# Differential attention on one Trainium2 core: all copies of turned weights on ScalarE, in the order in which TensorE makes them

## What is computed

```python
s = einsum('bqhcd,bkhcd->bchqk', q_blk, k) * scale     # c: two score maps per head
mask = cid[None, :] <= c_blk[:, None]
p = softmax(where(mask, s, NEG_INF), axis=-1)
w = p[:, 0] - lam * p[:, 1]
o = einsum('bhqk,bkhe->bqhe', w, v)                    # 4 heads, v is 128 wide
```

## Time and profile before

| | |
|---|---|
| median of 3 runs | 2430.82 us |
| the profiled execution | 2428.37 us |
| its span, first to last instruction | 2426.5 us |
| TensorE busy | 2216.3 us (91%) |
| VectorE busy | 783.8 us (32%) |
| ScalarE busy | 474.7 us (20%) |
| GpSimd busy | 308.9 us (13%) |
| mean granted clock of TensorE | 0.952 |

### The profile page before, as it was taken

The page is one execution under the profiler, slowest core; times in us unless marked ns, Lnnn a source line. Parts: engine busy times, 40 slices in busy tenths (PEclk is TensorE's granted clock), DMA queues, the critical chain, the costliest instruction groups (busy, mean ns, idle before and its releaser), DMA issues. The chain is left out here.

```text
span 2426.5 us, 33639 instructions
## 1 busy us (share of the span) xinstructions
PE 2216.3 (91%) x13491; PEld 1256.3 (52%) x13491; DVE 783.8 (32%) x1658; ACT 474.7 (20%) x885; POOL 308.9 (13%) x263
## 2 busy tenths in 40 slices
PE   8999997779949999999967999999976999999994
PEld 5778554555535545454434555555544554545541
DVE  7642245554361111111126344444243111111116
ACT  2222243331101000000003444441110000000001
POOL 7252000001101111111002000000101111101102
PEclk9999997889969999999988999999987999999998
DMA  4100001011259999989979111102119999999987
GB/s 154 37 36 1 20 1 70 1 33 43 69 202 399 420 419 420 416 337 409 411 300 309 51 39 39 32 11 53 56 53 392 416 417 420 420 376 372 417 367 297
DMA packets 148201, 529.82 MB, mean 218 GB/s; under 512 B 43875, under 2 KB 66947, under 8 KB 131665
## 3 DMA queue, kind: packets, MB, share of 16 engines
q1 hardware_dynamic: 127040, 493.66, 51.4%
q0 software_dynamic: 13312, 33.84, 3.7%
q10 hardware_dynamic: 7696, 0.19, 0.2%
HBM read 499.99 MB, written 39.98 MB: 223 GB/s over the span
## 5 line engine op out<-in xcount | busy, mean ns | idle before, releaser
L1864 PE MATMUL l_main_pgu<-l_w_ring,l_ex_xT 128*64 128x256 f32 (+1 forms) x4992 | 472.2, 384 | 11.3 <-DMA l_w_ring<-in_l_moe_w_gate 9.2
L1864 PEld LDWEIGHTS l_main_pgu<-l_w_ring,l_ex_xT 128*64 128x64 f32 (+1 forms) x4992 | 284.9, 128 | 187.9 <-issue 38.5
L1910 PE MATMUL l_main_py<-l_w_ring,l_ex_hT 128*64 128x512 f32 (+1 forms) x1248 | 231.9, 594 | 1.9 <-DVE l_ex_hT L1981 1.9
L1861 PE MATMUL l_main_pgu<-l_w_ring,l_ex_xT 128*128 128x512 f32 x384 | 170.1, 596 | 5.0 <-DMA l_w_ring<-in_l_moe_w_gate 5.0
L1977 DVE TENSOR_TENSOR l_ex_hid<-l_ex_sil,l_main_pgu 128x256 f32<-128x256 f32 (+1 forms) x76 | 35.2, 464 | 374.9 <-PE l_main_pgu L1864 277.7
L1981 DVE COPY l_ex_hT<-l_main_ph 128x256 f32<-128x256 f32 (+1 forms) x76 | 35.5, 467 | 366.4 <-PE l_main_ph L1885 366.4
L2322 PE MATMUL lru_pr<-h2T,lru_wz 128*128 128x352 f32 (+1 forms) x480 | 143.5, 459 | 10.8 <-ACTq L2377 10.8
L2340 PE MATMUL lru_pg<-h2T,lru_wz 128*128 128x512 f32 x320 | 148.7, 592 | 0.0
L1910 PEld LDWEIGHTS l_main_py<-l_w_ring,l_ex_hT 128*64 128x64 f32 (+1 forms) x1248 | 69.1, 127 | 132.1 <-issue 124.8
L2322 PEld LDWEIGHTS lru_pr<-h2T,lru_wz 128*128 128x128 f32 x480 | 92.1, 192 | 63.2 <-ACTq L2377 11.2
L1953 ACT ACTIVATE l_ex_sil<-l_main_pgu 128x256 f32<-128x256 f32 (+1 forms) x76 | 31.8, 418 | 468.2 <-PE l_main_pgu L1864 372.3
(11 more groups left out here) (459 smaller groups left out, 2810.6 us busy)
## 6 DMA issues: line engine op xcount, KB each, us to landing
l_w_ring<-in_l_moe_w_gate SPq DMA_DIRECT2D x64, 2048.0 KB, 24.8
l_w_ring<-in_l_moe_w_up SPq DMA_DIRECT2D x64, 2048.0 KB, 30.2
l_w_ring<-in_l_moe_w_down SPq DMA_DIRECT2D x64, 2048.0 KB, 31.7
l_y<-expert_rows SPq DMA_DIRECT2D x32, 512.0 KB, 8.1
h_rows<-H SPq DMA_DIRECT2D x24, 512.0 KB, 5.4
lru_wz<-in_l_w_in SPq DMA_DIRECT2D x20, 512.0 KB, 4.9
w_in<-in_l_w_in SPq DMA_DIRECT2D x4, 2048.0 KB, 9.5
H<-h_rows SPq DMA_DIRECT2D x16, 512.0 KB, 10.0
```

Of the source, the lines that this page charges most:

```text
L1861: last = pe.matmul(out[:], x[:, k, :], w[0][:, k, :], start=k == 0, stop=k == KD - 1)
L1864: last = pe.matmul(out[HALF * h + o:HALF * h + o + m, 0:256], x[:, k, it.at + o:it.at + o + m], w[n][:, k, 256 * h:256 * h + 256], start=k ...
L1910: last = pe.matmul(py[b][HALF * h + o:HALF * h + o + m, :], hT[:, c % 2, HALF * (c // 2) + o:HALF * (c // 2) + o + m], ws[n][:, c, 512 * h ...
```

## The change

The order of work changes in three places, all in `attention`:

- The copies leave VectorE. ScalarE makes every copy, group after group in the order in which TensorE turns them, with one semaphore (`w_copied`). Its round is now: copy of group 0 of unit u-1, first exponential of unit u+1, copy of group 1, second exponential, copy of group 2, `out(u-2)`.
- A copy is one instruction for the whole group. Where the group holds key tile 0, it copies 128 rows of that tile too, 112 of which were never written by a turn; so VectorE clears the first 128 columns of `turned_w` once at the start, and `meta_scores` waits for that (`tp_cleared`).
- v's products of a round stand all between the first `turn` and the first `weigh`; none stands before the `turn`.

```diff
             def meta_scores():
+                pe.wait_ge(tp_cleared, 1)
...
             def turn(u, j):
                 if n:
-                    pe.wait_ge((turned_a, turned_v)[(n - 1) % 2], (n - 1) // 2 + 1)
+                    pe.wait_ge(w_copied, n)
...
             def weigh(u, j):
-                pe.wait_ge((turned_a, turned_v)[n % 2], n // 2 + 1)
+                pe.wait_ge(w_copied, n + 1)
...
-                middle = (v_until[u + 1] + v_until[u + 2]) // 2
-                v_products(v_until[u + 1], middle)
                 for j in range(max(groups)):
                     if 0 <= u - LAG + 1 < U and j < groups[u - LAG + 1]:
                         turn(u - LAG + 1, j)
                     if j == 0:
-                        v_products(middle, v_until[u + 2])
+                        v_products(v_until[u + 1], v_until[u + 2])
...
+            def copy_turned(u, j):
+                if not (0 <= u < U and j < groups[u]):
+                    return
+                qi = units[u][1]
+                m, n = TILES[qi][1], first_group[u] + j
+                act.wait_ge(turned, n + 1)
+                if u >= 2:
+                    act.wait_ge(o_ready, u - 1)
+                k0, k1 = PER * j, min(PER * j + PER, qi + 1)
+                keys = P if k1 > 1 else N_META
+                act.copy(wT[u % 2][0:keys, k0:k1, 0:m], tp[0:keys, 0:k1 - k0, 0:m]).then_inc(w_copied, 1)
...
             for u in range(-1, U + LAG):            # ScalarE
-                if u + 1 < U:
-                    exps(u + 1, 0)
-                if 0 <= u - LAG + 1 < U:
-                    copies(act, act.copy, u - LAG + 1, 0, turned_a)
-                if u + 1 < U:
-                    exps(u + 1, 1)
+                for j in range(max(groups)):
+                    copy_turned(u - LAG + 1, j)
+                    if u + 1 < U and j < 2:
+                        exps(u + 1, j)
...
             do(dve.memset(ss[:], 0.0), wait=False)   # VectorE
+            dve.memset(tp[:, 0, :], 0.0).then_inc(tp_cleared, 1)
             do(dve.memset(o_sb[:, 0, :], 0.0))
...
                 if 0 <= u < U:
                     combine(u)
-                if 0 <= u - LAG + 1 < U:
-                    copies(dve, dve.tensor_copy, u - LAG + 1, 1, turned_v)
                 if 0 <= u - LAG - 1 < U:
                     square(u - LAG - 1)
```

More of the change, by code:

```diff
@@ L706, in attention @@
     sem = lambda n: K.sem("da_" + n)
-    (lexp_done, s_ready, mn_ready, exp_done, w_ready, turned, turned_a, turned_v, o_ready, o_copied,
+    (lexp_done, s_ready, mn_ready, exp_done, w_ready, turned, w_copied, tp_cleared, o_ready, o_copied,
      squared, dve_order, tail_done, tail_made, v_ready, v_copied) = map(sem, (
-        "lexp_done", "s_ready", "mn_ready", "exp_done", "w_ready", "turned", "turned_a",
-        "turned_v", "o_ready", "o_copied", "squared", "dve_order", "tail_done", "tail_made", "v_ready", "v_copied"))
+        "lexp_done", "s_ready", "mn_ready", "exp_done", "w_ready", "turned", "w_copied",
+        "tp_cleared", "o_ready", "o_copied", "squared", "dve_order", "tail_done", "tail_made", "v_ready", "v_copied"))
     ms_ready, sd_ready, on_ready, oT_ready, oT_copied = map(sem, ("ms_ready", "sd_ready", "on_ready", "oT_ready", "oT_copied"))
@@ L846, in _ @@
                 last.then_inc(oT_ready, 1)
[L848 to L865, removed]
         @block.scalar
```

## The result

The changed kernel takes 2368.61 us, the median of four runs (2363.71 to 2371.58), beside 2430.18 us before: ratio 0.9744, 95% interval 0.9722 to 0.9766. The profiled execution took 2371.58 us with a span of 2369.5, so it is 57.0 us shorter than the span before; the sum of the prediction said 51.7.

What follows compares the result with a forecast made beforehand. The order of work was taken as the bound, with TensorE waiting at `turn` in attention's long rounds. -33.4 + 2.2 - 21.0 + 0.2 + 0.3 = -51.7 us from 2428.4; 2379 us against the median, range 2371 to 2398.

Steps and rivals of the forecast that it cites:

- The waits at `turn`: Attention: with copies in TensorE's order, its waits for VectorE's and ScalarE's copies go, 28.8 + 4.6 = 33.4 us.
- ScalarE next: Rounds scoring 1040-key units: ScalarE is late next, TensorE waits for the exponential and `out`, 2.2 us added (0 to 3.6).
- VectorE: Attention: VectorE loses its copies, is not waited for afterwards, so this is worth nothing by itself.
- The low clock: Long rounds: low clock behind waits mostly goes, 22.7 us saved, 1.7 kept behind v's last copy, net 21.0 (0 to 24.2).
- The rival from the Trainium skill: Attention: short idle moments between matmul groups keep the clock falling, 21 us not gained; clock staying low: 2400 us, chance 0.12.
- The floor: Long rounds: TensorE's busy time at full clock, 109.4 - 22.7 = 86.7 us for 18 rounds, 4.8 us each.
- v's products: Short rounds: moving these products behind the turn is an exchange on TensorE's own list and costs nothing.
- The clearing: Start of attention: `meta_scores` waits for one more memset, clearing part of `turned_w`; 0.3 us added (0 to 0.6).
- What follows: After attention: w_out's load still has 90 us, so everything later moves up as a block.
- v's copy: End of the short rounds: the 1.9 us wait for the last copy of v stays, 0.2 us added as TensorE arrives sooner.

Runs made afterwards that it cites:

- copies alone moved: The changed kernel with v's products split again, half before the first turn and half behind it; 2373.41 us, ratio 0.9787 to the kernel before.
- v's copy moved up: The changed kernel with ScalarE's copy of a finished v tile behind the round's first exponential instead of behind `out`; 2365.45 us, again 2366.78 us.
- shared copies: The changed kernel with copies by turns on ScalarE and VectorE, each at its place in TensorE's order; 2385.45 us, ratio 0.9816 to the kernel before.
- exponential first: The changed kernel with unit u+1's exponential ahead of unit u-1's copy on ScalarE, all copies still there; 2391.75 us, ratio 0.985 to the kernel before.
- copies before the weights: The kernel before with VectorE's copies ahead of the next unit's weights, still behind both minima; 2395.01 us, ratio 0.9867.
- v's products moved: The kernel before with only v's products moved, all behind the first turn; 2426.03 us, ratio 0.9994.

## Why the prediction was right or wrong

**The waits at `turn`: right.** 33.4 us were to go and 33.35 went; no turn waits for a copy any more (one weighing of the last short units waits 0.4 us for one). The prediction put too much on the long waits, though: it had the low windows all "behind waits of 2 us and more", and four of the eleven, from 376.33, 383.15, 441.18 and 506.04 us, stood behind waits of 1.92, 1.45, 1.79 and 1.91 us. The two sides of the theory were tested apart: the order by turning ScalarE's list round, and the engine by sharing the copies again.

**ScalarE next: right.** 2.2 us were forecast for the 1040-key rounds; 1.7 came there and 0.14 once for a 912-key unit, in waits for the exponential of up to 0.5 us. The forecast had half of it as waits for `out`; in the long rounds none came.

**VectorE: too simple.** "It is not waited for afterwards, so this is worth nothing by itself" holds for VectorE's free time, but not for the place of its minima. With the copies in TensorE's order and half of them still on VectorE, some 12 us of the gain were missing.

**The low clock: right in kind, close in size.** 22.7 us were to go and 1.7 to come back behind v's last copy. What stayed differed by run: 3.4 or 9.8 us of low clock, and none with the copies alone moved. Three traces of the changed order have the same waits and differ in this alone: long rounds of 84.99, 86.50 and 89.49 us with 0, 3.4 and 9.8 us of it. So one busy microsecond at the low level costs 0.44 to 0.46 us here, 1.51 by 3.4 and 4.50 by 9.8. By the table below the low clock of the kernel before cost 22.9 us, and 1.5 us are still paid in the changed one: 21.4 us against 21.0 net.

The rival from the Trainium skill (TensorE: Matmul & The Clock Gate, "A second HAM failure mode: psum-queue depth-cycling") did not appear: with 1.8 us of small waits spread over 85 us the clock was 1.00 for all the long rounds in three traces (copies alone, and twice with v's copy moved up). No long round here shows the falling clock that this section describes without waits of a microsecond or more.

**The floor: wrong, and this is the step that failed.** The sum had TensorE's work in the long rounds at full clock as 109.4 - 22.7 = 86.7 us. It is 83.1 us: that is the busy time in the three traces at clock 1.00, alike to within 0.02. The prediction priced a wait at its idle time. But a wait also breaks the overlap of neighbours on TensorE. Round 22 shows it, at the high clock in both kernels and with the same 38 instructions, before and after:

```profile
430.00 1.35 PE L820 MATMUL weighed<-v_rows,w_cols 16*128 16x128 f32 x8
432.44 0.44 PE L804 MATMUL turned_w<-ident,w_rows 128*128 128x128 f32 x2 [1.09 <-ACT w_cols L865]
432.71 1.28 PE L820 MATMUL weighed<-v_rows,w_cols 128*128 128x128 f32 x10
433.93 0.70 PE L768 MATMUL scores<-kT,qT 64*128 64x512 f32 x2
```
```profile
404.61 1.35 PE L821 MATMUL weighed<-v_rows,w_cols 16*128 16x128 f32 x8
405.79 0.38 PE L805 MATMUL turned_w<-ident,w_rows 128*128 128x128 f32 x2
406.01 1.28 PE L821 MATMUL weighed<-v_rows,w_cols 128*128 128x128 f32 x10
407.22 0.70 PE L768 MATMUL scores<-kT,qT 64*128 64x512 f32 x2
```

The round lasts 6.42 us before and 5.10 after, a difference of 1.32 for a wait of 1.09. From the start of the weighing to the turns it is 2.44 us and 1.18, which is 0.17 more than the wait; from the turns to the next weighing 0.27 and 0.22. Everything else in the round is equal to 0.01 us. So the last products of the weighing end beside nothing, and the turns start into an empty engine: 0.22 us on top of the idle time.

Four kernels have 42 such waits in rounds that lie wholly at the high clock. Beside the same rounds of the kernel with the copies alone moved, these rounds are 8.6 us longer than their idle time explains, 0.2 us a wait. A wait elsewhere need not cost this: in the run with shared copies, four rounds with 1.3 to 1.7 us of waits ahead of scores were longer by the idle time alone. With 0.2 us a wait, the long rounds of the four kernels come out so, "low" being TensorE's busy time at the low clock:

```
                            long    busy   over 83.1   waits at turn   0.2 x waits   left    low   left per low
exponential first          108.2    92.5      9.4           14             2.8        6.6   13.4       0.49
copies before the weights  106.2    88.2      5.0           19             3.8        1.2    3.4       0.35
v's products moved         137.4   105.7     22.5           17             3.4       19.1   40.6       0.47
before                     142.0   109.4     26.3           17             3.4       22.9   48.4       0.47
```

So the price of the low clock was right (22.9 us, with 22.7 taken), and the 3.4 us of broken overlap are nearly all of the 3.6 us by which the floor was too high. The Trainium skill has a caution that bears on this (Perfetto Trace Analysis, "Identifying the Most-Contended Engine"): the busy share of matmuls is not a good measure of how close TensorE is to its limit, because pipelined instructions look smaller in the trace. The trace agrees: at the high clock the same 38 instructions of round 22 are busy for 5.10 us when they run on, and for 5.33 with the wait between them.

**v's products: wrong by 1.8 us.** The prediction had it that "an exchange of neighbours on its own list costs nothing". That held for the waits; but with one switch fewer between products and turns each of the rounds 1 to 15 is 0.1 to 0.2 us shorter.

**The clearing: right.** 0.3 us forecast; the memset took 0.17 us, TensorE waited 0.15, and round -1 grew by 0.24.

**What follows: right.** From the last `out` of attention to the end of the span it is 1901.9 us before and 1902.7 after.

Together: 3.4 us for the 17 waits of the long rounds and 0.4 for the two of the short ones, 1.8 for v's products, 0.4 for smaller waits, 0.4 for the clock and 0.3 for v's copy and the clearing make 6.7. Less 1.3, because the stage begins 0.3 us later and what comes behind the long rounds is 1.0 us longer, this is, to within 0.1, the 5.3 us between the forecast 51.7 and the 57.0 of the spans. The other 4.6 us of the first measurement's 61.6 are scatter: in the two later measurements the change is worth 53.7 and 59.7 us. On which side of the range's end the time falls is within that scatter: the second median, 2373.4 us, lies inside it. The range ended 2 us below the sum's own lowest value and had nothing for a floor that might be lower; a term taken from busy time needed a bound below itself.

## What to carry to other kernels

Look for the engine that waits in the middle of a round, and read in the other engine's list what stands ahead of the instruction that releases it; a copy that frees a buffer belongs where its producer and consumer meet it, ahead of work that is due a round later. But ask as well what that copy delays on its new engine: here ScalarE had room and VectorE did not. In this kernel a wait of TensorE between a weighing and a turn costs its idle time, 0.2 us of lost overlap, and, where waits of about 2 us recur, nearly half of the busy time at the low clock behind them; so even useless products in its place paid, by 0.3% here. Busy time that stands around waits is not a floor.

## What the runs showed of the hardware that was not expected

- TensorE's clock could be bought back with work that no one reads: 30.8 us of added products in the kernel before made its long rounds 9.7 us shorter.
- Behind the same wait of 1.9 us the changed kernel kept 3.4 us of low clock in two traces and 9.8 in a third, and none in the trace with the copies alone moved. That moves the stage by up to 4.5 us. Round -1 of attention likewise lasts 6.7 us in the changed kernel with 3.4 us of low clock in it and 8.2 to 8.3 with 6.8.
- A VectorE memset of 128 columns of PSUM takes 0.17 us.
- One change fewer between products of 512 columns and turns made rounds without idle time 0.1 to 0.2 us shorter.
- A wait between a weighing and the turns behind it cost 0.2 us more than the idle time that the trace shows (42 waits, 8.6 us, all at the high clock).
